# Norming the sample queries first, keeping the prompt roots for the softmax, and a separate buffer for the first half sequence's cache pages

## The chip, the cores and the metric

The kernel runs on one core of a Trainium2 chip. Its engines are TensorE (PE), VectorE (DVE), ScalarE (ACT), GpSimd (POOL) and SyncE (SP); each runs its own list of instructions in order and they meet through semaphores. SP issues the weight loads and the loads of cache A, POOL those of cache B. The metric is the device time of one run in microseconds, taken as the median of several runs.

## The reference

One step of a hybrid decoder layer in float32, for a prompt of 256 tokens and for 8 sample sequences of one new token each, with 1024 past tokens per sequence in paged caches. Cut to what matters:

```python
x = x + 0.5 * g1 * swiglu(mod1(rms_norm(x)))               # first FFN, D_FF = 2816
h = mod2(rms_norm(x)); proj = h @ w_in                      # [qA|kA|vA|qB|kB|vB|gA|gB]
q_a = rms_norm(q_a per head of 64, qn_moba); k_a likewise
q_b = rms_norm(q_b per half of 64, qn_diff); k_b likewise
s = q.k * 64**-0.5 - slope[head] * (q_pos - key_pos); masked; p = softmax(s)
# A: 8 heads, best 3 past blocks of 256 + own block;  B: 4 heads, p0 - lambda * p1, sub-norm
x = x + g2 * ((sig(gA) * yA + sig(gB) * yB) @ w_out)
x = x + 0.5 * g3 * swiglu(mod3(rms_norm(x)))               # second FFN
```

The shifts, scales and gates come from silu(c) @ w_ada, where w_ada is 1024 x 9216. The new k and v rows are outputs as well.

## The kernel before, in words

All 264 tokens (256 prompt, 8 sample) are the moving side of each product. A weight block is 1 MB: SP loads it into one of four buffers (raw), ACT rounds it to a high part (whi, L674), VectorE subtracts to get the low part (wlo, L981; fifteen halves of the k and v blocks are done by POOL, L629), and TensorE makes three products from the parts (L1482 to L1484): 24 products per half block. A function lo(filler(k)) or hi(filler(k)) does half k of the eight k and v blocks; kv_product(k) is its product.

**Start.** Four groups of w_ada columns are multiplied with the conditioning vectors (function ada, L1540). The first two come from the raw buffers, the other two from four buffers called early. Ahead of each of these four early parts TensorE does one idle_products(5, 1) (L1512), a product nobody reads; idle_products(5, 5) follows. The result goes through VectorE (mod_add, coefficients) into the first norm, after which the first FFN begins.

**Query projection.** Four blocks W_QK+0 to 3. After each, ACT copies the queries to qT and squares them; TensorE sums the squares over heads of 64 with a block-diagonal matrix (head_sum, L1697: two products of 264 columns); ACT takes roots for all 264 columns (head_root); VectorE inverts them (L1170) and multiplies them in (L1176).

**K stage.** The pages of the caches are read in half sequences: 4 pages x 128 tokens x 512 floats per cache, 1 MB for A and 1 MB for B. "Use" u = 0 to 15 are keys, 16 to 31 values. Three buffers per cache hold them (KVS = 3), the third lent: for A it is the fourth raw buffer. turn_keys(u) transposes use u on VectorE, A then B (L1201). The sample queries are spread on all partitions by small products (replicate_q, L1719), copied (L1301), and place_q(s) masks them into rows for sequence s (L1214). scores(u) multiplies (L1733), 32 products per cache. A load of use u waits until scores(u - 3) is done. Between these run the k and v blocks: kv_product, root of k (L791), k_norm (L1181, L1184), transposes of new k and v rows (k_turn, v_turn), outputs. The order on TensorE is: kv_product 0, head_sum(3), kv_product 1, k_sum(0), kv_product 2 and 3, k_sum(1), replicate_q, scores(0), kv_product 4, turns, scores(1), and so on; on VectorE: turn_keys(0), lo(filler(3)), the last query norm, lo(filler(4)), copy, place_q(0), place_q(1), then k_norm and turn_keys(1) and so on.

**V stage.** For each of eight steps c, TensorE multiplies values of two uses (L1844), half blocks of the gates (L1804 to L1806) and the prompt's own attention: prompt_scores (L1812, L1813), prompt_logits on VectorE (L1346 to L1349), prompt_exp on ACT (L878, L879), scaling (L1376 or L1378), transposes (L1870), output (L1892, L1893), and L1900 at steps 3 and 7. Then come the branch maps, w_out, and the second FFN.

Of the kernel before, what the change touches and what calls it, by code (L numbers as in the profile page):

```python
# [23 lines left out]
P = 128  # L24
D = 1024
KC = D // P
TP = 256
# [95 lines left out]
def _columns():  # L123
    at = 0
    for name, w in (("ident", 128), ("blockdiag", 128), ("ones", 128), ("half", 2), ("sel8", 14), ("perm", 176), ("sel4", 4), ("quad", 4), ("rowsum", 128),
                    ("negslope", 1), ("eps", 1), ("coef1", 1), ("coeflam", 1), ("rowA", 1), ("tri", 16),
                    ("dist", 384), ("distrow", 256), ("maskA", 8), ("maskB", 4)):
        CW[name] = (at, w)
        at += w
    return at  # L130
# [10 lines left out]
def constants():  # L141
# [37 lines left out]
    put("distrow", PAST - (128 * (4 * (k // 128) + k % 4) + 32 * tok[:, None] + 4 * (k % 32 // 4) + k % 128 // 32))  # L179
    put("maskA", np.arange(8)[None] == p[:, None] % 8)  # L180
# [29 lines left out]
def build(nc, A, O):  # L210
    ctx = ExitStack()
    with ctx:
# [37 lines left out]
        tmps = place("tmps", [P, 2, TS])  # L250
        region = at[0]
# [63 lines left out]

        osq = place("osq", [P, 4, T], where=[kT_at])
# [29 lines left out]
        s_proj, s_nsum, s_nvar, s_nrstd, s_qk = sem("proj_out"), sem("head_squares_summed"), sem("head_variance"), sem("head_rstd"), sem("qk_ready")  # L346
# [3 lines left out]
        s_qzero, s_qrep, s_qcopy, s_qrow = sem("q_rows_zeroed"), sem("q_replicated"), sem("q_copied"), sem("q_rows_ready")  # L350
        s_kv = [[sem(f"kv_landed{a}{s}") for s in range(KVS)] for a in "AB"]
# [88 lines left out]
        def load_half(eng, ab, cache, ids, half, use):  # L440


            for q in range(4):
                page = ids[4 * half + q]
                rows_ = kv_slot(ab, use)[q:P:4, :, :].rearrange("p t d -> p (t d)")
                eng.dma_start(rows_, cache[bass.ds(page, 1)].rearrange("a (j t) d -> (a j) (t d)", t=4)).then_inc(s_kv[ab][use % KVS], 16)  # L446

        def kv_landed(use):
            return 64 * (use // KVS + 1)
# [3 lines left out]
        def kv_load(eng, ab, use):  # L453
# [5 lines left out]
            if use == KVS - 1:  # L459
# [4 lines left out]
            if 0 <= prev < 16:  # L464
# [23 lines left out]
        def _(sp):  # L488
            def slot_free(key, shift=0):
# [58 lines left out]
            for use in range(KVS - 1):  # L548
# [41 lines left out]
        def _(pool):  # L590
# [13 lines left out]
            for use in range(KVS):  # L604
# [27 lines left out]
            for use in range(KVS, 4 * TS):  # L632
# [26 lines left out]
        def _(a):  # L659
# [26 lines left out]
            def head_root(u):  # L686

                a.wait_ge(s_nsum, u)
                if u > 1:
                    a.wait_ge(s_qk, u - 1)  # L690
                nc.scalar.activation(rstd[:, :, :], bank[:, 6:8, 0:T], ACT.Sqrt, bias=C("eps"), scale=1.0 / 64).then_inc(s_nvar, 1)
# [92 lines left out]
            def k_root(i):  # L784
# [4 lines left out]
                else:  # L789
                    a.wait_ge(s_qk, 4)  # L790
                nc.scalar.activation(rstd[:, i % 2, :], bank[:, 4, 0:T], ACT.Sqrt, bias=C("eps"), scale=1.0 / 64).then_inc(s_kroot, 1)  # L791

            def k_tokens(i):

                a.wait_ge(s_turn, i + 1)
                f0 = 128 * i
# [8 lines left out]
            def v_tokens(g, j):  # L805

                a.wait_ge(s_vturn, j + 1)
                f0 = 128 * j
# [17 lines left out]
            for u in range(4):  # L826
# [3 lines left out]
                if u:  # L830
                    head_root(u)
# [8 lines left out]
            for u in range(2 * TS + 2):  # L840
                if u < 16:
                    kind, i = kv_half(u)
                    (k_out if kind == "k" else v_out)(u, i)
                if u == 0:
                    head_root(4)
# [28 lines left out]
            def prompt_exp(c):  # L874
                for h in range(2):
                    a.wait_ge(s_plog, 2 * c + h + 1)
                    o = 16 * h + 16
                    nc.scalar.activation(plog[h][:, 0:128], plog[h][:, 0:128], ACT.Exp, bias=stat[:, o + 3:o + 4], accum_out=stat[:, o + 5:o + 6])  # L878
                    nc.scalar.activation(plog[h][:, 128:384], plog[h][:, 128:384], ACT.Exp, bias=stat[:, o + 4:o + 5],  # L879
# [91 lines left out]
        def _(v):  # L971
# [194 lines left out]
            nk = 0  # L1166

            def head_reciprocal(u):
                v.wait_ge(s_nvar, nk)
                dve.reciprocal(rstd[:, :, :], rstd[:, :, :]).then_inc(s_nrstd, 1)  # L1170

            def head_norm(u):
                v.wait_ge(s_nrstd, nk)
                dst = qT[:, 2 * u:2 * u + 2, :]
                g = 8 + u // 2
                dve.scalar_tensor_tensor(out=dst, in0=dst, scalar=misc[:, g:g + 1], in1=rstd[:, :, :], op0=ALU.mult, op1=ALU.mult).then_inc(s_qk, 1)  # L1176
# [10 lines left out]
            for u in range(4):  # L1187
                lo(W_QK + u + 1, 1)
                if u:
                    nk += 1  # L1190
                lo(W_QK + u + 2, 0)
                if u:
                    head_reciprocal(u - 1)
                    head_norm(u - 1)

            def turn_keys(u):

                for ab in range(2):
                    slot = kv_slot(ab, u)[:, :, :].rearrange("p q d -> p (q d)")
                    v.wait_ge(s_kv[ab][u % KVS], kv_landed(u))  # L1200
# [93 lines left out]
            turn_keys(0)  # L1294
            lo(*filler(3))
            nk += 1
# [9 lines left out]
            for u in range(2, 2 * TS + 2):  # L1306
# [6 lines left out]
                if u - 1 < 2 * TS:  # L1313
# [3 lines left out]
                if u == 12:  # L1317
                    v.wait_ge(s_mod, ADAS - 1)
# [661 lines left out]
```

## Time and profile before

| | |
|---|---|
| median of 3 runs | 785.14 us (782.84 to 785.8) |
| the profiled execution, its own time | 787.28 us |
| its span, first to last instruction | 785.6 us |
| TensorE busy, mean granted clock | 742.3 us (94%), 0.977 |
| VectorE busy | 480.9 us (61%) |
| ScalarE busy | 321.0 us (41%) |
| GpSimd busy | 124.1 us (16%) |
| moved by DMA | 209.53 MB, mean 267 GB/s |

The profiled execution took 1.7 us more than its span, and 2.1 us more than the median of the runs. The span can be cut as follows: start to 38.6 us, first FFN to 259.5, query projection to 286.7, K stage to 407, V stage to 524, branch maps and w_out to 584, second FFN to the end.

### The profile page before, as it was taken

How to read it: one execution, taken by the hardware profiler on the slowest of the kernel's cores; microseconds unless marked ns; L12 is line 12 of the kernel's file. 1: busy time of each engine (PE TensorE's matmuls, PEld its weight loads, DVE VectorE, ACT ScalarE, POOL GpSimd, SP SyncE). 2: the span in 40 equal slices, each digit the busy share in tenths (PEclk: the TensorE clock that was granted, in tenths of full speed). 3: DMA queues.
4: the chain of work that ended last, by engine and by line, in shares of the span. 5: the costliest groups of instructions: out<-in, count | busy, mean ns of one | idle time of the engine just before them, and what ended most of it. 6: DMA issues, size and time to landing. Idle time of an engine off the chain costs nothing.

```text
span 785.6 us, 17013 instructions
## 1 busy us (share of the span) xinstructions
PE 742.3 (94%) x6628; PEld 654.3 (83%) x6628; DVE 480.9 (61%) x692; ACT 321.0 (41%) x515; POOL 124.1 (16%) x179
## 2 busy tenths in 40 slices
PE   5999999999999998988878999999989999999997
PEld 2398898999998798877764666669979999999997
DVE  2654445455354998899987544667766465454551
ACT  1453333334343652333315543455445444444331
POOL 0000000002000302867863323210000000000000
PEclk9999999999999999999989999979999999999999
DMA  8967989988985855999999998995625655646530
GB/s 352 367 204 268 324 295 310 332 256 302 389 283 166 316 166 175 367 400 409 404 377 380 405 404 316 338 351 187 186 84 161 198 177 166 206 149 201 164 106 28
DMA packets 116520, 209.53 MB, mean 267 GB/s; under 512 B 6714, under 2 KB 100186, under 8 KB 104162
## 3 DMA queue, kind: packets, MB, share of 16 engines
q1 hardware_dynamic: 106784, 159.47, 59.1%
q0 software_dynamic: 9440, 49.02, 16.1%
q8 instruction: 46, 0.75, 0.4%
q14 instruction: 24, 0.20, 0.1%
q10 hardware_dynamic: 226, 0.10, 0.1%
HBM read 205.31 MB, written 3.24 MB: 265 GB/s over the span
## 4 chain that ended last, share of the span: by engine, by line
PE 76%; DVE 14%; DMA 4%; issue 2%; ACT 2%; SPq 1%; ACTq 0%; DVEq 0%; POOLq 0%
PE bank L1482 20%; PE bank L1483 19%; PE bank L1484 19%; PE bank L1540 3%; PE bank L1844 3%; DMA kvA<-in_cache_k_moba 2%; DMA kvA_lent<-in_cache_k_moba 2%; DVE kvB L1201 1%; DVE kvA L1201 1%; PE bank L1804 1%; PE bank L1733 1%; DVE wlo L981 1%; PE bank L1548 1%; PE bank L1805 1%; PE bank L1806 1%
## 5 line engine op out<-in xcount | busy, mean ns | idle before, releaser
L981 DVE TENSOR_TENSOR wlo<-raw,whi 128x1024 fp32r<-128x1024 f32 (+1 forms) x177 | 208.6, 1199 | 188.2 <-ACT whi L674 185.7
L1482 PE MATMUL bank<-hhi,whi 128*128 128x264 f32 x992 | 287.9, 290 | 5.5 <-DVE wlo L981 2.6
L1483 PE MATMUL bank<-hlo,whi 128*128 128x264 f32 x992 | 282.9, 285 | 0.0
L1484 PE MATMUL bank<-hhi,wlo 128*128 128x264 f32 x992 | 282.4, 285 | 0.0
L674 ACT ACTIVATE whi<-raw 128x1024 fp32r<-128x1024 f32 (+1 forms) x192 | 194.6, 1035 | 109.3 <-PE bank L1484 77.6
L1482 PEld LDWEIGHTS bank<-hhi,whi 128*128 128x128 f32 x992 | 188.5, 190 | 18.5 <-issue 15.1
L1483 PEld LDWEIGHTS bank<-hlo,whi 128*128 128x128 f32 x992 | 188.6, 190 | 0.2
L1484 PEld LDWEIGHTS bank<-hhi,wlo 128*128 128x128 f32 x992 | 187.8, 189 | 0.0
L1482 PE MATMUL bank<-ahi,whi 128*128 128x264 f32 x416 | 119.6, 288 | 0.4 <-DVE alo L1440 0.4
L1484 PE MATMUL bank<-ahi,wlo 128*128 128x264 f32 x416 | 118.1, 284 | 0.0
L1483 PE MATMUL bank<-alo,whi 128*128 128x264 f32 x416 | 117.8, 283 | 0.0
L1482 PEld LDWEIGHTS bank<-ahi,whi 128*128 128x128 f32 x416 | 78.2, 188 | 0.8 <-DVE alo L1440 0.6
L1483 PEld LDWEIGHTS bank<-alo,whi 128*128 128x128 f32 x416 | 78.2, 188 | 0.2
L1484 PEld LDWEIGHTS bank<-ahi,wlo 128*128 128x128 f32 x416 | 78.3, 188 | 0.0
L709 ACT ACTIVATE sil<-bank 128x528 f32<-128x528 f32 x22 | 13.5, 612 | 72.2 <-PE bank L1484 72.2
L446 POOL DMA_DIRECT2D kvB<-in_cache_k_diff x44 | 23.3, 530 | 112.3 <-issue 64.8
L629 POOL TENSOR_TENSOR wlo<-raw,whi 128x1024 fp32r<-128x1024 f32 x15 | 35.8, 2389 | 3.0 <-issue 2.6
L713 ACT ACTIVATE ahi<-act 128x528 f32 (+1 forms) x22 | 14.2, 645 | 54.0 <-DVE act L1067 54.0
L446 POOL DMA_DIRECT2D kvB<-in_cache_v_diff x44 | 23.3, 530 | 50.5 <-PE bank L1844 41.0
L1804 PE MATMUL bank<-hhi,whi 128*128 128x264 f32 x96 | 29.0, 302 | 0.0
L1805 PE MATMUL bank<-hlo,whi 128*128 128x264 f32 x96 | 27.6, 288 | 0.0
L1806 PE MATMUL bank<-hhi,wlo 128*128 128x264 f32 x96 | 27.5, 287 | 0.0
(258 smaller groups left out, 818.0 us busy)
## 6 DMA issues: line engine op xcount, KB each, us to landing
raw<-in_ffn_w_gate SPq DMA_DIRECT2D x22, 1024.0 KB, 5.4
raw<-in_ffn_w_up SPq DMA_DIRECT2D x22, 1024.0 KB, 5.5
raw<-in_w_ada SPq DMA_DIRECT2D x20, 1024.0 KB, 6.9
raw<-in_w_in SPq DMA_DIRECT2D x20, 1024.0 KB, 10.6
raw<-in_ffn_w_down SPq DMA_DIRECT2D x16, 1024.0 KB, 5.3
kvB<-in_cache_k_diff POOLq DMA_DIRECT2D x44, 256.0 KB, 6.4
kvA<-in_cache_k_moba SPq DMA_DIRECT2D x44, 256.0 KB, 8.6
kvA<-in_cache_v_moba SPq DMA_DIRECT2D x44, 256.0 KB, 6.9
```

Of the source, the lines that this page charges most:

```text
L446: eng.dma_start(rows_, cache[bass.ds(page, 1)].rearrange("a (j t) d -> (a j) (t d)", t=4)).then_inc(s_kv[ab][use % KVS], 16)
L629: nc.gpsimd.tensor_tensor(half_view(wlo[n % 2], key, t), half_view(raw[s], key, t), half_view(whi[n % 2], key, t).bitcast(F32), ALU.subtra ...
L674: nc.scalar.activation(half_view(whi[key[1] % 2], key, t), half_view(raw[s], key, t), ACT.Copy).then_inc(s_hi, 1)
L981: dve.tensor_tensor(half_view(wlo[key[1] % 2], key, t), half_view(raw[s], key, t), half_view(whi[key[1] % 2], key, t).bitcast(F32), ALU.su ...
L1482: mm(out, wh, xh, start=start, stop=False)
L1483: mm(out, wh, xl, start=False, stop=False)
L1484: return mm(out, wl, xh, start=False, stop=stop)
L1540: ins = mm(bank[32 * j:32 * j + 32, b, 0:n].rearrange("p (t a) -> p t a", a=32), csilu[:, kc, :], cols[:, :, j, :], start=(kc == 0), stop= ...
L1804: mm(out, wh, hhi[:, k, :], start=(k == 0), stop=False)
L1805: mm(out, wh, hlo[:, k, :], start=False, stop=False)
L1806: ins = mm(out, wl, hhi[:, k, :], start=False, stop=(k == KC - 1))
L1844: ins = mm(bank[32 * q:32 * q + 32, 4 + ab, :], wpad[half][:, q, ab, w0:w0 + 32], kv_slot(ab, use)[:, q, :], start=(half == 0 and c % 4 == ...
```

## The change

1. Queries. ACT now squares first and copies second, with the query gain applied in the copy. Only the 8 sample columns are normed: head_sum makes one 16-column product for their sums, and four products whose stationary side is a 128x128 piece of the squares and whose moving side has 2 columns, for the prompt's sums. After head_sum(3), ACT takes both roots (64 and 32 columns), VectorE inverts the 64 and scales the sample queries.
2. Prompt queries stay unnormed. At u = 12 of the K stage VectorE inverts their 32 columns of roots and multiplies the roots by the slopes. prompt_logits becomes two instructions instead of one (128 and 256 columns), and the exponential takes the inverse root as its scale.
3. Use 0 gets a buffer of its own in each cache, where v and k rows will lie later; the three others serve uses 1 to 31. Uses 0 to 3 are loaded ahead, use 4 waits for scores(1). Use 0's load waits for the last product of ada(3, 3). The fourth raw buffer is free for w_out after use 30 rather than 29.
4. Order. VectorE: turn_keys(0), norm of the sample queries, lo(filler(3)), lo(filler(4)), turn_keys(1), copy, place_q(0) and (1). TensorE: replicate_q directly behind k_sum(0); kv_product(3) behind scores(0). POOL does lo(filler(5)) ahead of the load of use 4.
5. The four idle_products(5, 1) at the start are gone; idle_products(5, 5) stays.

```diff
         def kv_slot(ab, use):
-            if use % KVS < KVS - 1:
-                return kv[ab][use % KVS]
-            return kv_lent[ab]
+            if use == 0:
+                return kv_first[ab]
+            return kv[ab][(use - 1) % KVS] if (use - 1) % KVS < KVS - 1 else kv_lent[ab]
...
             prev = use - KVS
-            if use == KVS - 1:
+            if use == 0:
+                eng.wait_ge(s_ada, ADA_N2 + 4)
+            if use == KVS:
...
-            if 0 <= prev < 16:
+            if 1 <= prev < 16:
                 eng.wait_ge(s_kS[ab], prev + 1)
...
-                    sp.wait_ge(s_pv, 2 * (4 * TS - 1 - (4 * TS - 1 - (KVS - 1)) % KVS - 16) + 1)
+                    sp.wait_ge(s_pv, 2 * (4 * TS - 1 - (4 * TS - 1 - KVS) % KVS - 16) + 1)
...
-            for use in range(KVS - 1):
+            for use in range(KVS):
                 kv_load(sp, 0, use)
             load_w(W_KV + 1)
             load_w(W_KV + 2)
-            kv_load(sp, 0, KVS - 1)
+            kv_load(sp, 0, KVS)
...
-            for use in range(KVS, 4 * TS):
+            lo(*filler(5))
+            for use in range(KVS + 1, 4 * TS):
                 kv_load(pool, 1, use)
...
+            def head_roots():
+
+                a.wait_ge(s_nsum, 4)
+                nc.scalar.activation(qnorm[:, :], bank[:, 7, 0:64], ACT.Sqrt, bias=C("eps"), scale=1.0 / 64).then_inc(s_nvar, 1)
+                nc.scalar.activation(qroot[:, 0, :], bank[:, 6, 0:32], ACT.Sqrt, bias=C("eps"), scale=1.0 / 64).then_inc(s_nvar, 1)
...
-                nc.scalar.activation(qT[:, 2 * u:2 * u + 2, :], src, ACT.Copy)
                 if u:
                     a.wait_ge(s_nsum, u)
-                nc.scalar.activation(sqb[:, :, :], src, ACT.Square).then_inc(s_proj, 1)
+                nc.scalar.activation(sqb[:, :, :], src, ACT.Square).then_inc(s_qsq, 1)
+                g = 8 + u // 2
+                nc.scalar.activation(qT[:, 2 * u:2 * u + 2, :], src, ACT.Identity, scale=misc[:, g:g + 1]).then_inc(s_proj, 1)
...
+            def sample_q_norm():
+
+                v.wait_ge(s_nvar, 1)
+                ch.link(dve.reciprocal(qnorm[:, :], qnorm[:, :]))
+                v.wait_ge(s_proj, 4)
+                dst = qT[:, :, TP:T]
+                dve.tensor_tensor(dst, dst, qnorm[:, :].rearrange("p (c s) -> p c s", s=TS), ALU.mult).then_inc(s_qk, 1)
+
+            def prompt_q_roots():
+
+                v.wait_ge(s_nvar, 2)
+                v.wait_ge(s_const_late, 16)
+                ch.link(dve.reciprocal(qroot[:, 2, :], qroot[:, 0, :]))
+                ch.link(dve.tensor_tensor(qroot[:, 1, :], qroot[:, 0, :], C("nslopes"), ALU.mult))
...
             turn_keys(0)
+            sample_q_norm()
             lo(*filler(3))
-            nk += 1
-            head_reciprocal(3)
-            head_norm(3)
             lo(*filler(4))
+            turn_keys(1)
             v.wait_ge(s_qrep, 1)
...
-                    ch.link(dve.scalar_tensor_tensor(out=plog[h][:, :], in0=C("dist"), scalar=-slope_of_row(j), in1=bank[:, h, 0:384], op0=ALU.mult, op1=ALU.add))
+                    for tb, (e0, e1) in enumerate(((0, 128), (128, 384))):
+                        q = 16 * tb + j
+                        ins = dve.scalar_tensor_tensor(out=plog[h][:, e0:e1], in0=C("dist", e0, e1), scalar=qroot[:, 1, q:q + 1], in1=bank[:, h, e0:e1],
+                                                       op0=ALU.mult, op1=ALU.add)
+                    ch.link(ins)
...
-                    if sc == 0 and q >= ADA_RING:
-                        idle_products(5, 1)
...
+                mm(bank[:, 7, 16 * u:16 * u + 16].rearrange("p (t s) -> p t s", s=TS), C("blockdiag"), sqb[:, :, TP:T], start=True, stop=True)
                 for t in range(2):
-                    ins = mm(bank[:, 6 + t, 0:T], C("blockdiag"), sqb[:, t, :], start=True, stop=True)
+                    for tb in range(2):
+                        c0 = 16 * tb + 2 * (2 * u + t)
+                        ins = mm(bank[:, 6, c0:c0 + 2], sqb[:, t, P * tb:P * tb + P], C("half"), start=True, stop=True)
...
-                if 2 <= u < 16:
+                if 3 <= u < 16:
                     kv_product(u + 1)
...
-                if u == 2:
+                if u == 1:
                     replicate_q()
-                    pe.wait_ge(s_nvar, 4)
+                    pe.wait_ge(s_nvar, 2)
...
                 if u >= 2:
                     scores(u - 2)
+                if u == 2:
+                    kv_product(3)
```

## Rows read from the trace of the kernel before

**Rows 1.** Stretches: per engine busy us and count, then granted clock, DMA share, GB/s.
```profile
36.90:38.60 1.70, 0.00 (x0) 0.00 (x0) 1.70 (x3) 1.70 (x4) 0.00 (x0) 1.00 1.10 348
40.00:43.40 3.40, 3.40 (x18) 3.40 (x17) 3.40 (x9) 3.02 (x3) 0.00 (x0) 0.51 0.91 299
259.50:265.90 6.40, 6.36 (x52) 6.11 (x48) 5.68 (x14) 4.75 (x8) 0.43 (x1) 1.00 0.98 390
265.90:292.00 26.10, 25.35 (x197) 24.86 (x197) 25.49 (x19) 14.93 (x23) 3.51 (x6) 1.00 0.67 218
304.00:307.00 3.00, 3.00 (x66) 2.80 (x57) 2.96 (x3) 0.00 (x0) 0.00 (x0) 0.62 0.02 5
305.70:320.00 14.30, 14.30 (x234) 12.97 (x226) 14.26 (x9) 4.88 (x14) 10.00 (x12) 0.98 0.84 277
320.00:402.90 82.90, 71.12 (x1103) 61.94 (x1101) 77.36 (x105) 24.87 (x60) 62.79 (x75) 0.96 1.03 405
430.00:470.00 40.00, 39.99 (x346) 26.84 (x338) 21.25 (x53) 19.74 (x58) 12.78 (x24) 1.00 1.03 405
```

**Rows 2.** Chain that ended last, start stage: start us, us, what.
```profile
24.39 0.86 PE bank L1512 x2
...
31.40 1.04 PE bank L1540 x8
```

**Rows 3.** DMA: issue at 5.6 us and its landing; issue at 16.4 (last number: landing).
```profile
L522 SPq DMA_DIRECT2D early<-in_w_ada x1: 445/445/445, 5.6 to 5.6; - x1
DMA to landing us min/median/max: 23.2/23.2/23.2
...
raw<-in_ffn_w_gate SPq DMA_DIRECT2D x1, 1024.0 KB, 15.4
```

**Rows 4.** Timeline, ACT: first weight halves, a small activation, w_out's halves.
```profile
9.84 0.24 ACT L728 ACTIVATE csilu<-bank 128x72 f32<-128x72 f32 x1 [6.06 <-PE bank L1556]
34.90 1.99 ACT L674 ACTIVATE whi<-raw 128x1024 fp32r<-128x1024 f32 x2
545.83 2.01 ACT L674 ACTIVATE whi<-raw 128x1024 fp32r<-128x1024 f32 x2 [6.24 <-PE bank L1484]
```

**Rows 5.** Chain, small products and scores: start us, us, what.
```profile
269.79 0.89 PE bank L1697 x4
470.52 1.92 PE bank L1900 x16
303.62 3.22 PE bank L1733 x64
310.61 1.88 PE bank L1733 x64
```

**Rows 6.** Timeline, TensorE, around the last head sum.
```profile
289.67 1.05 PE L1697 MATMUL bank<-sqb,const 128*128 128x264 f32 x4
293.45 0.61 PE L1678 MATMUL bank<-sqb,const 128*128 128x264 f32 x2
```

**Rows 7.** Timeline, VectorE: a turned use begins, the instruction after it, the placed queries.
```profile
289.72 2.31 DVE L1201 STREAM_TRANSPOSE kvA<-kvA 128x2048 f32<-128x2048 f32 x1
...
294.14 1.18 DVE L981 TENSOR_TENSOR wlo<-raw,whi 128x1024 fp32r<-128x1024 f32 x1
...
302.99 0.93 DVE L1214 TENSOR_TENSOR qrow<-qrep,const 128x32 f32<-128x32 f32 x8
```

**Rows 8.** Timeline, VectorE, turned keys that waited for a landing.
```profile
332.75 2.31 DVE L1201 STREAM_TRANSPOSE kvA_lent<-kvA_lent 128x2048 f32<-128x2048 f32 x1 [2.11 <-DMA kvA_lent<-in_cache_k_moba]
402.87 2.31 DVE L1201 STREAM_TRANSPOSE kvA<-kvA 128x2048 f32<-128x2048 f32 x1 [1.31 <-DMA kvA<-in_cache_k_moba]
```

**Rows 9.** Timeline, SP: issues of uses 3 and 4 of cache A.
```profile
305.74 9.04 SPq L446 DMA_DIRECT2D kvA<-in_cache_k_moba  x8
```

**Rows 10.** Timeline, VectorE, the prompt's logits and a split pair.
```profile
466.10 0.56 DVE L1346 SCALAR_TENSOR_TENSOR plog<-const,bank 128x384 f32<-128x384 f32 x1 [0.37 <-PE bank L1813]
475.19 0.75 DVE L1376 SCALAR_TENSOR_TENSOR plog<-plog,stat,plog 128x128 f32<-128x128 f32 x2
```

More of the change, by code:

```diff
@@ L179, in constants @@
     put("distrow", PAST - (128 * (4 * (k // 128) + k % 4) + 32 * tok[:, None] + 4 * (k % 32 // 4) + k % 128 // 32))
+    put("nslopes", np.broadcast_to(np.array([-slope_of_row(j) for j in range(16)] * 2)[None], (P, 32)))
     put("maskA", np.arange(8)[None] == p[:, None] % 8)
@@ L250, in build @@
         tmps = place("tmps", [P, 2, TS])
+        qnorm = place("qnorm", [P, 64])
+        qroot = place("qroot", [P, 3, 32])
         region = at[0]
@@ L314, in build @@
         last_ada = [place(f"last_ada{e}", [P, UNIT], where=[(o + 31) // 32 * 32]) for e, o in enumerate(last_at)]
+        kv_first = [place("kvA_first", [P, 4, 512], where=[vtok_at]), place("kvB_first", [P, 4, 512], where=[gT_at])]
         osq = place("osq", [P, 4, T], where=[kT_at])
@@ L350, in build @@
         s_qzero, s_qrep, s_qcopy, s_qrow = sem("q_rows_zeroed"), sem("q_replicated"), sem("q_copied"), sem("q_rows_ready")
+        s_kv_first = [sem(f"kv_first_landed{a}") for a in "AB"]
         s_kv = [[sem(f"kv_landed{a}{s}") for s in range(KVS)] for a in "AB"]
@@ L430, in kv_slot, with kv_sem @@
         def kv_slot(ab, use):
-            if use % KVS < KVS - 1:
-                return kv[ab][use % KVS]
-            return kv_lent[ab]
+            if use == 0:
+                return kv_first[ab]
+            return kv[ab][(use - 1) % KVS] if (use - 1) % KVS < KVS - 1 else kv_lent[ab]
+        def kv_sem(ab, use):
+            return s_kv[ab][(use - 1) % KVS] if use else s_kv_first[ab]
         def page_ids(eng, s):
@@ L445, in load_half @@
                 rows_ = kv_slot(ab, use)[q:P:4, :, :].rearrange("p t d -> p (t d)")
-                eng.dma_start(rows_, cache[bass.ds(page, 1)].rearrange("a (j t) d -> (a j) (t d)", t=4)).then_inc(s_kv[ab][use % KVS], 16)
+                eng.dma_start(rows_, cache[bass.ds(page, 1)].rearrange("a (j t) d -> (a j) (t d)", t=4)).then_inc(kv_sem(ab, use), 16)
         def kv_landed(use):
-            return 64 * (use // KVS + 1)
+            return 64 * ((use - 1) // KVS + 1) if use else 64
         held = [None, None]
@@ L603, in _ @@
             pool.wait_ge(s_ptab, 16)
-            for use in range(KVS):
+            for use in range(KVS + 1):
                 kv_load(pool, 1, use)
@@ L630, in lo @@
                                         ALU.subtract).then_inc(s_lo, 1)
-            for use in range(KVS, 4 * TS):
+            lo(*filler(5))
+            for use in range(KVS + 1, 4 * TS):
                 kv_load(pool, 1, use)
@@ L795, in k_tokens @@
                 a.wait_ge(s_turn, i + 1)
+                if i == 0:
+                    a.wait_ge(s_kS[1], 1)
                 f0 = 128 * i
@@ L807, in v_tokens @@
                 a.wait_ge(s_vturn, j + 1)
+                if j == 0:
+                    a.wait_ge(s_kS[0], 1)
                 f0 = 128 * j
@@ L876, in prompt_exp @@
                     a.wait_ge(s_plog, 2 * c + h + 1)
[L877 to L879 removed]
+                    o, j = 16 * h + 16, 2 * c + h
+                    nc.scalar.activation(plog[h][:, 0:128], plog[h][:, 0:128], ACT.Exp, bias=stat[:, o + 3:o + 4], scale=qroot[:, 2, j:j + 1],
+                                         accum_out=stat[:, o + 5:o + 6])
+                    nc.scalar.activation(plog[h][:, 128:384], plog[h][:, 128:384], ACT.Exp, bias=stat[:, o + 4:o + 5], scale=qroot[:, 2, 16 + j:17 + j],
                                          accum_out=stat[:, o + 6:o + 7]).then_inc(s_pexp, 1)
@@ L1317, in _ @@
                 if u == 12:
+                    prompt_q_roots()
                     v.wait_ge(s_mod, ADAS - 1)
@@ L1841, in _ @@
                         use = 16 + 2 * c + half
-                        pe.wait_ge(s_kv[ab][use % KVS], kv_landed(use))
+                        pe.wait_ge(kv_sem(ab, use), kv_landed(use))
                         for q in range(4):
```

44 lines of the change are left out of this document (11 added, 33 removed).

## The prediction

> **What bounds the kernel now.** I read the stretches first. From 38.6 to about 287 us and in the second FFN TensorE sets the pace; in the query projection it is busy 25.35 of 26.1 us although VectorE is just as full (25.49) [rows 1]. The K stage is different: from 320 to 402.9 us TensorE has 11.8 us of holes, VectorE is busy 77.36 of 82.9 us, and the DMA engines run without a pause at 405 GB/s (share 1.03) [rows 1]. So the second view is the start of turned keys. Use 5 waited 2.11 us for its landing at 332.75, use 15, the last, waited 1.31 us at 402.87 [rows 8]. Between these two the chain goes through VectorE, but at both ends a landing decides, with the DMA at its ceiling. I therefore take the DMA as what ends the K stage, with VectorE close behind (1.3 us). In the V stage TensorE is full (39.99 of 40) and the DMA too [rows 1]. Last I read the chain at the start: it alternates idle products (0.86 us) and w_ada products until 32.4, then enters VectorE [rows 2].
>
> **The sum is made against the profiled execution (787.28 us) and carried over to the median of the runs, 785.14, which is 2.1 lower.**
>
> **1. Start: four idle products go.** They and the four w_ada parts stand alternately on the chain, some 8 us of TensorE time from 24.39 to 32.44 [rows 2]. At most 4 us could go. But the last early part was issued at 5.6 and landed 23.2 later, at 28.8 [rows 3]; its products take 1.04 [rows 2], so the end moves from 32.44 to about 30.0: 2.4 earlier. Next in line is the first FFN block: issued 16.4, landed 15.4 later at 31.8 [rows 3]; ACT wants it at 34.90 [rows 4], after the change at 32.5, so it is just in time. From there TensorE is the bound, and the 2.4 is carried to the K stage. The doubt is TensorE's clock. Before, an idle stretch of 36.9 to 38.6 is followed by 40.0 to 43.4 at granted clock 0.51, the 1.2 GHz level, which costs half of it, 1.7 us [rows 1]. The change keeps that hole (all moves together) and opens a new one of about 1.4 us before 28.8. A second slow stretch would cost up to 1.7, and the present one could vanish, worth as much. Bounds: -4.1 to 0, taken -2.4. The Trainium skill, "TensorE: Matmul & The Clock Gate", section "Part 1: The HAM clock gate", says that the gate follows how busy the array has lately been and falls to half rate after idleness. That speaks against taking filler products out; by it the start could give back most of what it wins (it is a rival below), while the only slow stretch the rows show there is the one at 40.0 to 43.4.
>
> **2. Query projection.** What goes: four inversions of 528 columns on VectorE with their multiplications, and four root activations on ACT. In the first three turns TensorE hides them (it has 0.75 us of holes in 26.1 [rows 1]), so they save nothing there; the fourth belongs to step 4. What comes on TensorE: head_sum was 4 instructions in 0.89 us; now 2 plus 8. The nearest row is L1900, also 128x128 stationary with few columns: 16 in 1.92, 0.12 each [rows 5]. So 1.2 per head_sum, +0.3 each, +0.9 for three in a TensorE-bound stage. Bounds: 0 below, if the 2-column products cost no more in all than the 264-column ones did; above, 0.24 each at half clock, 2.4 per head_sum, +4.5 for three.
>
> **3. Loads ahead.** SP and POOL started uses 0 and 1 right after the first FFN; now use 0 waits for the end of ada at 259.5, and on both queues uses 1 and 2, use 3 of cache B and the next weight block (SP) stand behind it, on POOL also the zeroing of the query rows (wanted only at 303). That is 4.2 MB through each queue, 8.4 MB at 390 GB/s [rows 1], 21.5 us, done near 281 to 282. ACT wants that block at about 284. Cover 2 us; beyond it ACT still has slack of some 3 us before the query squares. Use 3 follows before 290. I cost it at nothing.
>
> **4. When does scores(0) start?** Before: VectorE copies the replicated queries, places them at 302.99, and scores(0) starts at 303.62 [rows 5, 7]. After, in order: head_sum(3) starts 289.67 + 0.9 = 290.6, ends 291.8. ACT: root of 64 columns 0.25 (as L728) [rows 4], second root 0.2, k copy and square 0.6, weight half 1.0: 293.9. VectorE's lo(filler(3)) ends 295.2. TensorE's kv_product(1) ends at 291.8 + 2.9 = 294.7 (289.67 + 0.89 to 293.45) [rows 5, 6]; ACT takes 0.7 for copy and square, 0.5 for k's root, 1.0 for the next half: 297.0. lo(filler(4)) ends 298.2. Then turn_keys(1), new in this place: two transposes, 4.4 (289.72 to 294.14) [rows 7]: 302.6. Copy and first placement, 0.9 to 1.0: 303.6. So scores(0) starts where it did, at 303.6: the inversions are gone, and the transposition has taken their room. TensorE has nothing from 299.3 to 303.6, 4.3 us against 1.85 before.
>
> **5. When does the DMA resume?** Before, use 3's load was issued at 305.74, in scores(0) [rows 9]. Now uses 0 to 3 are in and use 4 waits for scores(1). Scores(1) comes after scores(0) (3.2, as before, where 1.3 of it is low clock: the next pair took 1.88 [rows 5]), two k/v products of 2.9, turns 0.65: 303.6 + 9.7 = 313.3, against 310.61 [rows 5]. Its A part ends 1.05 later, issue near 314.4. The DMA does nothing between. Account in DMA time: before, from 305.7 to 320 it moved 277 of 405 GB/s, 4.5 us lost of 14.3 [rows 1], so its full-rate start is 310.2. After: 314.4 plus 1.3 from issue to traffic (305.74 to 307, the stretch to 307 carried 5 GB/s [rows 1]) is 315.7; less the 2.1 MB of use 3 already there, 5.2 us at 405 GB/s, is 310.5. K stage: +0.3 to +0.4, head_sums included. Bounds: -4.4 if VectorE were the bound (rival), +2.7 if the delay of scores(1) passes in full.
>
> **6. Prompt logits.** One instruction of 0.56 becomes two; a pair of 128 and 256 columns took 0.75 [rows 10]: +0.2 per head. Two exponentials per head stay two. The chain of waits goes through these instructions at steps 0, 4 (466.10 [rows 10]) and 6, two heads each: +1.2. Bounds 0 (TensorE and DMA are both full in the V stage) to 3.2 (all 16 heads). The inverse roots at u = 12 take some 0.55 of VectorE, under the DMA. POOL's lo(filler(5)) comes earlier, and hides as before. w_out's first block loads about 7.5 us later (use 30 rather than 29), near 513, and with 15 us to its landing, as the first FFN block had [rows 3], is in at 528; ACT wants it at 545.83 [rows 4]: nothing.
>
> **Sum:** -2.4 + 0.4 + 1.2 = -0.8, so 786.5 for a profiled execution and 784.3 for the median.
>
> **Rivals.**
> - *VectorE paces the K stage.* For it: the chain between the two landings, 77.36 of 82.9 busy. Then its lead counts, one turned use that is done before the queries are placed, 4.4 us [rows 7]. Total -2.4 - 4.4 + 1.2 = -5.6: 779.5. Against it: the two waits at the ends and the full DMA. 0.22.
> - *The start gives nothing* because the clock falls in the thinned stretch: -0.8 + 2.4 = +1.6: 786.7. 0.14.
> - *Slower: TensorE's clock stays low after the longer wait before scores(0).* Scores(0), two products, turns and scores(1) all follow a 4.3 us hole; I counted 1.3 us of low clock, as before. Low throughout up to scores(1), the 8.35 us from scores(0) on (1.9 + 5.8 + 0.65) become 16.7, where I have 9.7: +7.0, and the DMA resumes by so much later: 785.14 - 0.8 + 7.0 = 791.3. Each further slow stretch costs 1.7; the kernel turns slower by over 0.5% if scores(1) starts later than 318.0 (4.7 more than my 313.3). Against it: full clock came back within 3.4 us at 43.4 [rows 1]. 0.12.
> - *As summed*, 0.52; its own range 781.5 to 787.
>
> **Numbers.** 0.5% (3.9 us) is about what a measurement tells from no change: faster is below 781.2, slower above 789.1. Faster: most of the first rival and a tail of the main case, 0.27. Slower: 0.12. The rest 0.61. The range reaches just past the VectorE case at the low end, and over the start rival with another slow stretch at the high end: 779.0 to 788.5.
>
> **What would show it.** First FFN product 2.4 earlier, near 36.3; no second stretch of clock 0.5 before it. Head sums of 1.2 us. Scores(0) near 301.2 (303.6 less 2.4), TensorE idle 4 us before. DMA traffic near zero between the landing of use 3 and scores(1), then 405 GB/s to the last landing of K pages near 401. If that landing comes well before 399, VectorE was the bound; if its wait for landings vanishes altogether, too. Pairs of logits 0.75. It would be wrong if weight block W_KV+1 lands after 287, if use 0's home delays the new rows, or if the clock in 300 to 315 is low for more than 3.4 us.

## The result and the profile after

The changed kernel takes 787.74 us (median of 11 runs, 784.9 to 790.93) against 784.66 for the kernel before on the same chip (11 runs): ratio 1.0044 [1.0023, 1.0065]. It is 0.44% slower, inside the 0.5% that I called no change, but its interval lies wholly above 1. I had forecast 784.3 from 785.14, 0.8 faster.

The profiled executions lie at opposite ends of their runs (787.28 of before is 2.6 over its median here, 784.9 of after 2.8 under), so I profiled an unchanged copy of before once more (label e8 below, 782.52 us, clock 0.987), and read after against both. Each row runs from the mark of the row above to the first product of the stage or instruction that it names, us:

| stretch | before | before again | after | after less again | forecast |
|---|---|---|---|---|---|
| start to query projection | 259.54 | 259.55 | 255.21 | -4.34 | -2.4 |
| to scores(0) | 44.08 | 44.08 | 44.03 | -0.05 | 0 |
| to scores(1) | 6.92 | 5.64 | 10.16 | +4.52 | +2.7 |
| to scores(15) | 94.70 | 93.61 | 92.62 | -0.99 | -2.4 |
| to V stage | 12.08 | 11.52 | 11.52 | 0 | 0 |
| values of use 16 to values of use 31 | 96.18 | 96.18 | 98.57 | +2.39 | +1.2 |
| to the end of the span | 272.09 | 270.26 | 271.08 | +0.82 | 0 |
| span | 785.59 | 780.84 | 783.19 | +2.35 | -0.8 |

One pair of profiles is a thin base for a few microseconds. The K stage of before was profiled three times (both executions and e1 below), with 145.7, 143.3 and 146.1 us from the projection's first product to scores(15); that of the changed kernel three times too (after, e2 and e3), with 146.8, 149.0 and 146.8. The means are 2.5 us apart, the pair in the table 3.5. The 2.39 us of the values stand firmly: the nine profiles with the split logits have 98.3 to 99.0, the four of before's kind 96.2 to 96.3. The last stretch is not the change's: nine of all fourteen profiles have 270.2 to 270.3 us there.

The start first: the chain of after (start us, us, what), then TensorE's timeline there.

```profile
20.64 3.77 PE bank L1564 x16
...
26.86 2.77 DVE work L1022 x8
...
34.62 1.23 DVE wlo L996
...
35.94 0.36 PE bank L1500
```

```profile
28.58 1.06 PE L1556 MATMUL bank<-early,csilu 128*32 128x512 f32 x8 [1.47 <-DMA early<-in_w_ada]
```

The idle products have left the chain, and from 24.4 us on it runs through VectorE and no longer through w_ada products. The last early part waits 1.47 us for its landing, and the first FFN product starts at 35.94 instead of 38.68.

Now the stretches of after that answer to [rows 1]: columns as there.

```profile
34.20:35.90 1.70, 0.00 (x0) 0.00 (x0) 1.70 (x3) 1.70 (x4) 0.00 (x0) 1.00 1.09 348
38.00:41.40 3.40, 3.40 (x30) 3.40 (x30) 3.40 (x8) 2.29 (x3) 0.00 (x0) 1.00 1.09 348
261.60:287.70 26.10, 25.38 (x213) 25.41 (x214) 15.28 (x13) 12.27 (x19) 5.99 (x10) 1.00 1.01 384
299.20:302.90 3.70, 3.66 (x65) 3.27 (x66) 3.67 (x7) 0.00 (x0) 0.00 (x0) 0.54 0.00 0
302.90:309.40 6.50, 6.50 (x54) 6.26 (x54) 6.46 (x5) 0.61 (x2) 0.00 (x0) 1.00 0.01 3
309.40:315.00 5.60, 5.60 (x95) 5.20 (x94) 3.86 (x6) 2.40 (x8) 2.81 (x5) 1.00 0.52 157
320.00:402.00 82.00, 70.41 (x1093) 60.88 (x1092) 77.72 (x103) 25.75 (x62) 61.46 (x72) 0.96 1.03 406
430.00:470.00 40.00, 38.81 (x311) 26.21 (x314) 22.36 (x57) 20.92 (x55) 11.08 (x21) 1.00 1.03 405
```

The same 1.7 us hole stands ahead of the first FFN, yet no half clock (1.2 GHz) follows at 38.0; that is worth 1.6 us of the start beside the 2.7. VectorE is relieved in the query projection (15.28 of 26.1 us, 25.49 before) and TensorE is as full as it was. From 299 to 309 the DMA engines move nothing, and from 320 they run at 406 GB/s, as before.

Timelines of after, first TensorE, then VectorE, ACT and SP, where the chain runs between head_sum(3) and scores(1):

```profile
286.09 0.29 PE L1710 MATMUL bank<-sqb,const 128*128 128x16 f32 x2
286.23 1.03 PE L1714 MATMUL bank<-const,sqb 128*128 128x2 f32 x8
...
294.26 0.61 PE L1694 MATMUL bank<-sqb,const 128*128 128x264 f32 x2
299.24 1.76 PE L1750 MATMUL bank<-kvA_first,qrow 128*32 128x128 f32 x32 [4.38 <-DVE qrow L1227]
...
309.40 1.08 PE L1750 MATMUL bank<-kvA,qrow 128*32 128x128 f32 x32
```

```profile
293.55 2.30 DVE L1214 STREAM_TRANSPOSE kvA<-kvA 128x2048 f32<-128x2048 f32 x1
295.78 2.27 DVE L1214 STREAM_TRANSPOSE kvB<-kvB 128x2048 f32<-128x2048 f32 x1
...
298.39 1.21 DVE L1227 TENSOR_TENSOR qrow<-qrep,const 128x32 f32<-128x32 f32 x8
...
318.77 2.31 DVE L1214 STREAM_TRANSPOSE kvA<-kvA 128x2048 f32<-128x2048 f32 x1 [5.52 <-DMA kvA<-in_cache_k_moba]
```

```profile
281.07 1.06 ACT L686 ACTIVATE whi<-raw 128x1024 fp32r<-128x1024 f32 x1 [2.46 <-DMA raw<-in_w_in]
```

```profile
310.69 2.45 SPq L455 DMA_DIRECT2D kvA<-in_cache_k_moba  x4
```

ACT waited 2.46 us for the landing of a weight block (W_KV+1), which it used from 281.07. TensorE stands idle 4.38 us until the queries are placed, behind turn_keys(1). SP issues use 4 at 310.69, when scores(1) has ended for A. VectorE, which had worked ahead, then waits 5.52 us for use 4: the lead that it won before scores(0) is handed back there.

The V stage: the prompt's logits of one head in VectorE's timeline, in after and in a kernel with one instruction (e3), each with the instruction that follows.

```profile
463.04 0.74 DVE L1361 SCALAR_TENSOR_TENSOR plog<-const,qroot,bank 128x128 f32<-128x128 f32 x2 [0.37 <-PE bank L1832]
463.81 0.55 DVE L1364 TENSOR_REDUCE stat<-plog 128x3 f32<-128x384 f32 x1
```

```profile
463.49 0.55 DVE L1359 SCALAR_TENSOR_TENSOR plog<-const,bank 128x384 f32<-128x384 f32 x1 [0.37 <-PE bank L1828]
464.08 0.55 DVE L1360 TENSOR_REDUCE stat<-plog 128x3 f32<-128x384 f32 x1
```

The pair takes 0.74 us from its first start to its last end, the single one 0.55 to 0.56: 0.18 more per head, and the next instruction starts later by as much (0.77 and 0.59 us behind the first start).

### The profile page after: what moved, and what is told of

Same layout as the page of the kernel before. It is cut to its first block, busy times and chain, and to the rows that moved or that the text cites. A ratio compares the mean times of both kernels' runs of the same rounds, so it can differ in the third digit from the quotient of the medians.

```text
span 783.2 us, 17057 instructions
## 1 busy us (share of the span) xinstructions
PE 735.7 (94%) x6644; PEld 650.4 (83%) x6644; DVE 469.8 (60%) x704; ACT 322.4 (41%) x513; POOL 123.6 (16%) x179
## 4 chain that ended last, share of the span: by engine, by line
PE 74%; DVE 17%; DMA 3%; issue 2%; ACT 2%; SPq 0%; ACTq 0%; DVEq 0%
PE bank L1500 20%; PE bank L1501 19%; PE bank L1502 19%; PE bank L1556 3%; PE bank L1863 2%; DVE kvA L1214 2%; DVE kvB L1214 2%; DMA kvA<-in_cache_k_moba 2%; DVE wlo L996 2%; PE bank L1750 1%; PE bank L1564 1%; DMA crow<-in_c_rows 1%; DVE plog L1361 1%; PE bank L1823 1%; DVE kvB_lent L1214 1%
## 5 line engine op out<-in xcount | busy, mean ns | idle before, releaser
L1502 PE MATMUL bank<-hhi,wlo 128*128 128x264 f32 x992 | 281.6, 284 | 0.0
L724 ACT ACTIVATE ahi<-act 128x528 f32 (+1 forms) x22 | 14.2, 646 | 53.8 <-DVE act L1082 53.8
L1214 DVE STREAM_TRANSPOSE kvA<-kvA 128x2048 f32<-128x2048 f32 x10 | 23.0, 2300 | 8.6 <-DMA kvA<-in_cache_k_moba 8.6
L1086 DVE TENSOR_TENSOR alo<-act,ahi 128x528 f32 (+1 forms) x22 | 15.6, 708 | 19.3 <-ACT ahi L724 19.3
```

The costliest lines, as they stand in the source:

```text
L1214: dve.transpose(slot, slot).then_inc(s_kT[ab], 1)
L1502: return mm(out, wl, xh, start=False, stop=stop)
```

## The experiments

Eleven kernels, and the one before once more. "K stage" is here the time from the query projection's first product to scores(15), read from one profile of each. Ratios are to the kernel before, run on the same chip.

**e1, e2: idle products.** e1 is before without the four, e2 is after with them.

```diff
                     if sc == 0 and q >= ADA_RING:
-                        idle_products(5, 1)
```

> The kernel before with one part of the change alone: the four idle products at the start are out. Theory 1 (the start is a gain of 2.4 us, and what made the changed kernel slower lies later): 2 to 3 us faster than before, first FFN product near 36.0 us instead of 38.7. Theory 2 (the idle products held the clock, and the profiled execution of the changed kernel, with full clock up to the K stage, was a lucky one): the first product is also near 36.0, but a stretch of half clock follows or precedes it in most executions, and the time is that of before within 1 us, or up to 2 us slower.

> The changed kernel with the four idle products put back. It is the mirror of the run before. Theory 1: 2 to 3 us slower than the changed kernel (ratio to before near 1.007). Theory 2: no slower than the changed kernel, perhaps 1 to 2 us faster (ratio 1.002 to 1.004).

e1: 782.63, ratio 0.9981 [0.9959, 1.0002]. e2: 789.38, 1.0084 [1.0052, 1.0116], 3.1 us (plus or minus 3.0) above after. In the profiles the first FFN block starts 1.94 earlier in e1 than in before (36.74), 2.96 later in e2 than in after (38.90). So the start gains, by 1.5 to 3 us in time, though e1's interval just reaches 1. Over all profiles the first FFN product starts at 38.6 to 39.2 us in the four kernels with the idle products and at 35.9 to 37.5 in the ten without, 2.1 us earlier on average.

**e3: one instruction for the prompt's logits.** It leaves the root out of the ALiBi term.

```diff
-                        ins = dve.scalar_tensor_tensor(out=plog[h][:, e0:e1], in0=C("dist", e0, e1), scalar=qroot[:, 1, q:q + 1], ...
+                    ch.link(dve.scalar_tensor_tensor(out=plog[h][:, :], in0=C("dist"), scalar=-slope_of_row(j), in1=bank[:, h, 0:384], ...
```

> The changed kernel with the prompt's logits made by one instruction of 384 columns per head again instead of two. It leaves out that the ALiBi term is multiplied by the query's root, so the prompt's distances weigh wrongly. It measures the term of the V stage: expected 1.2 us faster than the changed kernel (bounds 0 and 3). If instead most of the 3 us by which the changed kernel is slower come from this term, its ratio to before is 1.000 to 1.001; if they come from elsewhere it is 1.003.

786.19, 1.0027 [1.0007, 1.0047]: the times alone do not separate it from after (0.0017, plus or minus 0.0029). The profile does: from the values of use 16 to those of use 31 it takes 96.66 us, after 98.57, before 96.18. 1.9 of the 2.4 us lost there are the split.

**e4: after with three buffers**, the change's order kept. Use 3 waits for scores(0).

```diff
-            if use == 0:
-                return kv_first[ab]
-            return kv[ab][(use - 1) % KVS] if (use - 1) % KVS < KVS - 1 else kv_lent[ab]
+            if use % KVS < KVS - 1:
+                return kv[ab][use % KVS]
+            return kv_lent[ab]
```

> The changed kernel with three buffers per cache as before: uses 0 to 2 are loaded ahead and use 3 waits for scores(0); everything else as changed. If the DMA ends the K stage (my reading), the buffer for use 0 is worth the 5.2 us of DMA time less the later resumption: scores(0) is again near 299, use 3 is issued there near 301 rather than 305.7, so this kernel is about 1 to 3 us slower than the changed one. If VectorE paced the K stage, it is within 1 us of the changed kernel. If use 0's late load cost something, it is faster.

787.97, 1.0066 [1.0044, 1.0089]. My account gave use 3's early load 5.2 us; taking it away cost 1.7 (plus or minus 2.4) in time, and 0.6 in the K stage (147.39, after 146.81).

**e5, e6, e7: the orders of before put back into after**: TensorE's product 3 ahead of scores(0) (e5), VectorE's turn_keys(1) behind the two place_q (e6), both, with the three buffers of e4 (e7).

```diff
-                if 3 <= u < 16:
+                if 2 <= u < 16:
                     kv_product(u + 1)
...
-                if u == 2:
-                    kv_product(3)
```

```diff
             lo(*filler(4))
-            turn_keys(1)
...
             place_q(1)
+            turn_keys(1)
```

> The changed kernel with kv_product(3) on TensorE ahead of scores(0), as it stood before; nothing else. In the changed kernel's trace TensorE waits some 4 us ahead of scores(0) and scores(1) comes 10.2 us after it instead of 6.9. Theory P (the loss of the K stage is this order: the hole, the half clock behind it and the later resumption of the DMA): scores(0) stays at 44.0 us after the first query product, scores(1) comes 2.9 to 3.3 us earlier, the last turned use too, and the kernel is 2.5 to 4 us faster than the changed one, near or below before. Theory Q (the loss is spread: small head-sum products and later steps): within 1 us of the changed kernel.

> The changed kernel with turn_keys(1) on VectorE behind place_q(0) and place_q(1) instead of ahead of them; TensorE's order as changed. Theory P: scores(0) starts 4.2 us earlier (39.8 after the first query product), with no hole ahead of it; scores(1) follows 7 to 8 us later, 5 us earlier than in the changed kernel; the DMA takes up use 4 as much earlier, so up to 5 us are saved in the K stage: 3 to 5 us faster than the changed kernel, ratio to before 0.998 to 1.001. If VectorE paced the K stage, the transposition is only moved and the gain is under 1 us.

> The changed kernel with the three buffers and with the two orders (VectorE's turn_keys(1) inside the loop, TensorE's kv_product(3) first) of before: so of the change in the K stage only the norm of the sample queries is left, with the head sums, the two-instruction logits and the start without idle products. scores(0) near 42.7 after the first query product against 44.1 before, use 3 issued as much earlier: K stage 1.3 us faster than before; with the start at -2 and the logits at +2 the total is 1 to 2 us faster than before. If the norm itself is what costs the K stage its 3 us, it is as slow as the changed kernel.

e5 782.19, 0.9988 [0.9971, 1.0004]; e6 782.66, 0.9993 [0.9975, 1.0011]; e7 782.70, 0.9993 [0.9977, 1.0009]. Either order alone brings back what the change lost: 0.0056 (plus or minus 0.0027) for e5, 4.4 us. In the profiles scores(1) starts 54.19 us behind the projection in after, 49.40 in e5, 48.12 in e6 and e7, and the K stage takes 146.81, 143.37, 142.47 and 141.95.

**e8: before once more**, unchanged, for its profile.

> The kernel before once more, for a second profile of it. The first had 11 stretches of half clock, 37.5 us in all, where its 25 timed runs have 24.5 us on average. Expected: the same lengths of the stretches that hold no low clock (first query product to scores(0) 44.1, first FFN 219.3 plus what low clock adds, scores(0) to scores(1) 6.9), and less low clock in all; if the stretch at 40.0 is missing, the first FFN takes 219.3 instead of 220.9.

782.52; its stretches stand in the table above and below.

**e9: no inversion of k's root**, in e5. Eight inversions of 1.8 us go from VectorE; k is multiplied by its root instead, so that part of the computation is left out.

```diff
-                dve.reciprocal(rstd[:, i % 2, :], rstd[:, i % 2, :]).then_inc(s_krecip, 1)
-                v.wait_ge(s_krecip, i + 1)
```

> The kernel of e5 (product 3 ahead of scores(0), four buffers) without VectorE's inversion of the root of k's norm: 8 instructions of 1.8 us and their waits go; k is then multiplied by its root, which is the part left out. Theory that VectorE paces the K stage: proj to scores(15), 143.4 us in the profile of e5, comes 5 to 12 us shorter, and the time is 775 to 779 us (ratio 0.985 to 0.994); waits of VectorE on transfers grow, since they are what comes next. Rival, that the transfers end the K stage: the stage stays within 1 us of 143.4 and the ratio within 0.997 to 1.000, with the 14 us that are gone turned into waits on transfers.

782.58, 0.9988 [0.9967, 1.0009]: nothing. The K stage takes 143.25 (e5 143.37). The waits of VectorE for pages of cache A in the three buffers' own tile, 300 to 420 us, in e5 and then e9 (us in total, times, longest):

```profile
DVE kvA L1214 <- DMA kvA<-in_cache_k_moba: 4.1, 3, 2.2
```

```profile
DVE kvA L1212 <- DMA kvA<-in_cache_k_moba: 11.5, 3, 6.3
```

With the lent buffer's waits (1.5 and 1.4 us), waits for pages grew from 5.6 to 12.9 us, so 7.3 of the 14.1 us of inversions turned into waits. The rest came back as longer small instructions of VectorE: the eight multiplications of k took 1143 ns on average for 793, the placements of queries 327 for 212; what lengthened them is not shown. VectorE does not pace this K stage; I had leaned to that when I wrote this expectation, and it fell.

**e10: the hole filled.** After with idle products of TensorE where it stands still ahead of scores(0).

```diff
+                if u == 2:
+                    idle_products(3, 5)
```

> The changed kernel with its order kept (product 3 behind scores(0)), but with idle products of TensorE, some 4.3 us, where it otherwise stands still ahead of scores(0). Theory that the low clock there is what the hole costs beside the order: no low stretch between 299 and 310, scores(0) to scores(1) 8.6 us in place of 10.2, and the time 1 to 2.5 us under the changed kernel's (ratio to before 1.001 to 1.003). Rival, that only the order counts: scores(0) to scores(1) may shrink, but the ratio stays at 1.0044 within 0.0015.

785.79, 1.0032 [1.0016, 1.0048], against after's 1.0044: not separated (0.0012, plus or minus 0.0026). The profile shows no low clock there, and scores(0) to (1) in 8.55 us in place of 10.16, but the K stage is as long (146.76 against 146.81). The low clock costs 1.6 us locally; that it costs any of the time is not shown. Nor did the stage gain from scores(1) being 1.6 us earlier.

**e11: e7 with the fourth buffer**, thus e5 and e6 together.

```diff
-                if 3 <= u < 16:
+                if 2 <= u < 16:
                     kv_product(u + 1)
...
             place_q(1)
+            turn_keys(1)
```

> The changed kernel with both orders of before put back (product 3 ahead of scores(0), turn_keys(1) behind the two place_q), and its four buffers kept: e7 with a fourth buffer. Theory that VectorE paces the K stage: the fourth buffer gives 0 to 0.6 us, so 782.1 to 782.8 us and a ratio of 0.998 to 1.000. Rival, that the transfers' lead of one use counts: 779.5 to 781 us (ratio 0.995 to 0.997), the few us that the prediction credited to the fourth buffer.

782.08, 0.9974 [0.9958, 0.9989], the fastest of all, and the only interval wholly under 1. Against e7 the fourth buffer is worth 0.0019 (plus or minus 0.0022), which may be nothing; 5.2 us would be 0.0066, and are excluded. The time is the one that the expectation's VectorE theory gives, but e9 speaks against that theory, and the next part shows another reason.

**e12: the mirror.** Before with product 3 moved behind scores(0), as the change has it.

```diff
-                if 2 <= u < 16:
+                if 3 <= u < 16:
                     kv_product(u + 1)
...
                     scores(u - 2)
+                if u == 2:
+                    kv_product(3)
```

> The kernel before with one edit, kv_product(3) moved from ahead of scores(0) to behind it: the mirror of e5. Theory that this order is the larger part of the loss: scores(0) to scores(1) goes from 5.7 to 6.9 us to 8.6 to 11.5, proj to scores(15) gains 2.5 to 4.5 us, and the ratio is 1.003 to 1.005. Rival, that the order costs only beside the early turn_keys(1) and the changed loads: ratio within 0.999 to 1.002.

786.36, 1.0041 [1.0022, 1.0061]: this one edit of order makes before as slow as after. Scores(0) to (1) takes 10.89 us, the K stage 148.42.

**Where the fourth buffer's lead goes.** Stretches around scores(1), one fence per kernel. Before again (three buffers): scores(0) to (1), the 5.6 us behind it, then scores(1) to (15).

```profile
303.63:309.27 5.64, 5.64 (x95) 5.20 (x95) 5.61 (x7) 0.22 (x1) 2.75 (x5) 1.00 0.50 166
309.27:314.87 5.60, 5.33 (x92) 4.84 (x92) 5.56 (x4) 2.22 (x7) 4.05 (x6) 1.00 1.00 338
...
309.27:402.88 93.61, 80.95 (x1275) 70.78 (x1274) 90.42 (x112) 30.85 (x77) 70.05 (x82) 0.96 1.03 399
```

After, scores(0) to (1) and (1) to (15) (four buffers):

```profile
299.24:309.40 10.16, 10.16 (x118) 9.53 (x118) 10.09 (x11) 0.61 (x2) 0.00 (x0) 0.83 0.01 2
309.40:402.02 92.62, 81.01 (x1275) 70.83 (x1274) 82.82 (x109) 30.43 (x76) 68.16 (x81) 0.96 1.00 389
```

e7 (three buffers) and e11 (four), the same three stretches as for before:

```profile
299.35:305.00 5.65, 5.65 (x95) 5.21 (x94) 5.61 (x4) 1.92 (x4) 3.98 (x5) 1.00 0.48 129
305.00:310.60 5.60, 5.60 (x95) 5.20 (x94) 5.60 (x4) 2.40 (x8) 3.28 (x6) 1.00 0.97 364
...
305.00:398.83 93.83, 80.78 (x1275) 70.69 (x1274) 88.06 (x112) 31.23 (x77) 69.44 (x83) 0.96 1.03 401
```

```profile
299.98:305.63 5.65, 5.65 (x96) 5.21 (x95) 5.61 (x4) 1.93 (x4) 2.39 (x1) 1.00 0.01 3
305.63:311.23 5.60, 5.60 (x95) 5.20 (x94) 5.56 (x5) 2.40 (x8) 2.81 (x5) 1.00 0.52 149
...
305.63:399.93 94.30, 82.98 (x1276) 73.08 (x1275) 88.41 (x113) 31.15 (x77) 68.50 (x82) 0.93 1.00 384
```

e4 (three buffers, the change's order), scores(0) to (1) and 5.6 us on:

```profile
300.79:311.48 10.69, 10.69 (x118) 9.83 (x118) 10.07 (x11) 0.61 (x2) 2.14 (x4) 0.78 0.56 192
311.48:317.08 5.60, 5.60 (x95) 5.21 (x94) 4.00 (x6) 2.40 (x8) 2.79 (x5) 1.00 0.53 164
```

With three buffers and scores(1) close behind scores(0), use 3 travels between the two and is still on its way when use 4 is released: no gap, and 316 to 364 GB/s in the next 5.6 us (before, before again, e1, e7). With four, it came earlier, the DMA engines then have nothing to do up to scores(1), and must start from zero: 135 to 170 GB/s in the same 5.6 us (all eight profiles with four buffers). So in e7 0.73 MB (5.65 us x 129) and 2.04 MB (5.60 x 364) move in these two stretches, in e11 0.02 and 0.83: the four-buffer kernel gives back 1.92 of the 2.1 MB that it was ahead. In e4 and e12 the long stretch from scores(0) to scores(1) lets use 3 land, and the gap is there with three buffers too (164 and 132 GB/s behind it).

## Why the prediction was wrong, point by point

**The bound was read rightly, as far as the runs go.** "I take the DMA as what ends the K stage": in e9 VectorE loses 7 us of busy time and the stage stays, and from 320 us to the last landing the DMA engines run at 405 to 406 GB/s in before and after alike. This refutes the rival that VectorE paces the stage for the kernel with four buffers. With three, VectorE is nearer to the edge: in before again it waits for pages only 2.0 us in the stage, and no run takes work from it there. The amount moved from the start up to scores(15) (GB/s times length of each stretch, summed) is 124.2 to 124.9 MB in nine profiles (before, before again, after, e5, e7, e9 to e12). That alone does not name the bound, since what must have landed by then is the same whatever paces the stage; together with the full rate it says how a delay counts.

**The step that failed is 5, in the term "less the 2.1 MB of use 3 already there, 5.2 us at 405 GB/s".** What preceded it held: scores(0) 44.03 us behind the projection (44.1 forecast by "303.6"), TensorE idle 4.38 (4.3), scores(1) 54.2 behind it (53.8), use 4's issue 1.3 behind scores(1) (1.1). Then I set the delay of scores(1) against the early load in full and came to +0.4. But the load that is moved ahead had lain in before mostly in time in which the DMA had no other work, between scores(0) and the end of scores(1), and it also bridged the restart. With both, little of the credit is left: the delay of scores(1) against before again is 4.5 us and the stage 3.5 longer, a credit of 1.0; after against e4 gives 0.6, e11 against e7 nothing. What is left is mostly the delay of scores(1). On the means of three profiles each, +2.5, the step's upper bound, "+2.7 if the delay of scores(1) passes in full", was much nearer than the +0.4 taken; against the one profile that I reckoned with it is +1.1.

That the stage follows scores(1) is seen over all kernels, columns: scores(1) and scores(15), both in us behind the projection:

```
e7 48.1 142.0 | e11 48.1 142.4 | e6 48.1 142.5 | e9 49.4 143.3 | e5 49.4 143.4
before again 49.7 143.3 | before 51.0 145.7 | e1 51.2 146.1 | e10 52.6 146.8
e3 54.0 146.8 | after 54.2 146.8 | e4 54.7 147.4 | e12 55.0 148.4 | e2 55.4 149.0
```

A straight line through them rises 0.84 us per us, with three buffers or four, and leaves at most 1.1. The points are single profiles, and e10 against after, 1.6 us apart in scores(1) and equal at scores(15), shows how much of a single step can be lost in the scatter.

**Step 6 was sized too small:** +1.2 forecast, +2.4 in the profile; 1.9 of it is the split (e3). The price per head was right (0.2, measured 0.18), the count of six heads on the path was not: 1.9 over 0.18 is about ten of the sixteen. The exponentials cost 0.09 us more each as well (medians 494 and 587 ns, 402 and 493 in before again), which I had left out; e3 has them too, and is 0.5 us over before. The Trainium skill, "ScalarE: Activation LUTs", section "What ACT_TABLE_LOAD costs", gives about 93 ns for each operand of an activation that is read from a column instead of standing in the instruction, and the trace agrees (92 and 94 ns).

**Step 1** held: 2.1 us at the first FFN product on average, 2.7 in after, for 2.4 forecast, and 1.5 to 3 in time. "The start gives nothing" is refuted, but its mechanism is there. By the rule that I quoted from the Trainium skill, "TensorE: Matmul & The Clock Gate", section "Part 1: The HAM clock gate", thinning the fillers could cost. In five of the ten profiles without them (e1, e3, e4, e6, e7) a stretch at 0.50 did appear at 28.9 to 30.3, at the new hole, and in none of the four with them. In these five the hole ahead of the last w_ada part was 1.95 to 2.36 us long; after, e5, e9 and e11 had 1.04 to 1.58 and kept full clock, but so did e10 with 2.79. It falls on the last w_ada part, which is on the chain there and took 1.2 to 1.9 us instead of 1.06: a cost of 0.15 to 0.9 us. On the other side the stretch near 40 us, worth 1.6, stood in three of the four and in one of the ten.

**Steps 2 and 3** held in time: head_sum 1.01 us on the chain (0.13 and 0.88; 1.2 forecast), and the stretch to scores(0) unchanged. But the block that I feared late was late: ACT waited 2.46 us for its landing, until 281.07, where "done near 281 to 282" less the 4.3 us of the start had meant 277 to 278. ACT's slack took it up.

**The rival of the low clock** went half its way: the 3.7 us behind scores(0)'s start were at 0.54, scores(1) came at 309.4, far short of the 318.0 from which it decides, and e10 does not show that it costs time. Half clock in the whole run (from each run's granted clock) is 31 us on average in after and 23 to 25 in before. As the explanation of the loss it does not do: e11 has 30 and is the fastest, e10 has 25 and is slower than before. Within one kernel, though, runs with 1 us more of it are about 0.2 us longer, so a share of up to some 1.5 us (an estimate from these numbers) stays open.

**The carry-over.** I reckoned against one profiled execution and took its difference to the median for constant. Its K stage holds half-clock stretches at 302.9 and 337.0 that before again lacks, and is 2.4 us longer (145.7 and 143.3). Only a second profile of before shows this.

With the measured terms, -2.3 (start, the mean of e1's 1.5 and e2's 3.1), +2.5 (K stage, means of three profiles) and +1.9 to 2.4 (logits), the sum is +2.1 to +2.6; with the K stage against before again alone, +3.5, it is +3.1 to +3.6. The medians say +3.1, with an interval of 1.8 to 5.1 by the ratio. The terms are consistent with that and no finer than 1 us.

## What to carry to other kernels

A transfer moved ahead earns only what it takes out of the stretch in which the DMA engines are full. Where it used to run in a gap that stays, or to bridge one, it earns nothing and opens a restart: count megabytes up to each landmark in both kernels, and look at the GB/s behind each release. When a stage must move a fixed amount of data and runs at the full rate, look for the release that starts the flow. Here this was scores(1). One product of 2.9 us on TensorE or one transposition of a use, 4.4 us on VectorE, placed ahead of it cost 3.4 and 4.3 us of the K stage (after against e5 and e6), though either engine had slack in the stage; the two together cost hardly more than the larger alone (4.4, after against e11). And take a second profile of the unchanged kernel before a sum of a few microseconds is built on one.

## What the runs showed of the hardware

Stretches of half clock (granted 0.50, the 1.2 GHz level) lasted 3.4 or 6.8 us, at most 10.2, apart from the one that ends each span, and lay at other places in another execution of the same kernel: before has one at 302.9 and one at 337.0, before again neither. At the start, before again and e1 (no idle products), stretches of 3.4 us:

```profile
39.80:43.20 3.40, 3.40 (x18) 3.40 (x17) 3.40 (x10) 3.16 (x3) 0.00 (x0) 0.50 0.97 303
```

```profile
30.10:33.50 3.40, 3.40 (x8) 1.50 (x5) 2.67 (x9) 1.54 (x3) 0.00 (x0) 0.50 1.10 348
39.80:43.20 3.40, 3.40 (x30) 3.40 (x29) 3.06 (x5) 1.66 (x2) 0.00 (x0) 1.00 0.71 227
```

The stretch near 40 us, in the first FFN, where it costs 1.6 us, stood in three of the four profiles with the idle products and in one of the ten without them (e11, at 37.9). The fillers did not keep the clock up there, while those near 30 us stood only without fillers. Behind a 4.4 us hole of TensorE ahead of scores(0), all four profiled kernels that have it (after, e2, e3, e4) show 3.4 or 6.8 us of half clock; with the hole filled (e10) there is none. Behind the 1.85 us hole of before's order it stood in two of three profiles (before and e1, not before again).

After a full stop of the DMA engines, the first 5.6 us behind the release of use 4 carried 132 to 170 GB/s, in ten profiles; with an earlier load still under way it was 316 to 364, in four. At the full 405 GB/s the difference is worth 2 to 3 us.
